# Broadcasting position rows in another stage, and clipping index scores in their banks

## The chip, the cores and the metric

The kernel runs on one core of one Trainium2 chip. The time is device microseconds of one execution. A core has a tensor engine (PE, whose weight loads are listed as PEld), a vector engine (DVE), a scalar engine (ACT), GpSimd (POOL), and SyncE (SP), which here only issues DMA. Each engine works through its own queue in order; semaphores tie the queues together. PE writes into eight banks of PSUM; everything else lies in SBUF or in device memory.

## The reference, cut to what matters

Three transformer blocks run one after the other on a 1024 x 1024 sequence in float32. Block one normalises its input, projects it, passes part of it through a depthwise convolution and a state-space scan, and does differential attention. Block two has a gated unit, a band attention, a memory attention, and a sparse attention (DSA) that keeps, for each query, the 256 best keys by an index score. Block three is a windowed attention beside a convolution, and an MLP. The change touches two computations.

The first is data that depends on relative position: for the band attention and for the sparse attention, a row of biases per head.

```python
s = jnp.where(valid[None, :, None, None, :, :], s + bias[None, None], -jnp.inf)   # band
bias = t5_table[t5_bucket(idx - qpos[None, :, None])]                             # sparse
```

The second is the index score, a weighted sum over eight index heads of the clipped product of an index query and the index keys:

```python
logits = jnp.einsum('bqhd,bsd->bqhs', iqb.astype(jnp.float32), ikf) * (IDX_DIM ** -0.5)
score = jnp.einsum('bqhs,bqh->bqs', jax.nn.relu(logits),
                   iwb.astype(jnp.float32) * (IDX_HEADS ** -0.5))
_, idx = lax.top_k(score, k_sel)
```

## The kernel before, in words

Every engine has one program: a list of stages (`gpsimd_program`, `sync_program` and so on at the end of the file), each stage a function such as `pe_norm` or `pool_conv`. Nothing is planned at run time; the order in each queue is the order in which the functions issue. Float32 products are made from three products of split parts: a matrix is split into a high part (ACT copies it) and a low part (DVE or POOL subtracts), and each product is hi x hi + hi x lo + lo x hi.

**DMA.** SP starts the loads and POOL the stores, through a class `Transfers` with eight lanes of semaphores each: transfer n waits, on the issuing engine, until transfer n-8 has landed. The order of all stores is written out in `store_order` so that any engine can wait for a named store.

**The norm stage** (`*_norm`). Eight tiles of 128 positions are normalised. Then z is projected in 16 pieces (`("nat", n)`, n = 0 to 15; product L688), which ACT takes out of the banks into four buffers and POOL stores (`saved(n)`, tensor `z_spill`). Beside the last of these PE makes the position rows (`pe_rows`), ACT takes them out, SP writes them to device memory (`("row", ...)`), and POOL broadcasts each row to 128 copies with a copy from device memory to device memory (`pool_rows`: `band_wide`, 1536 KB, and `toe_wide`, 2304 KB). The attention stages of block two read these wide tensors through a skewed pattern (`attention_tables`).

After the 16 pieces, v and g are projected with seven products in place of eight (`SEVEN`, product L735). The weights of each product come in two units. For unit u SP loads raw blocks (`sp_unit`, waits for PE's unit u-4, and for the first unit of kind 5, which is unit 4, for the z stores 12 to 15, whose buffers lie under the ones that it fills), POOL may subtract two blocks (`pool_unit`), ACT makes the high part (L385), DVE the low part (L394), PE multiplies: 24 matmuls per unit. Finished tiles of v and g are stored by POOL (`finished`), and all engines wait for the last of these stores before the next stage (`norm_over`).

**The convolution stage** (`*_conv`). Thirteen column tiles of 128 (items; `b1item_stage`) are loaded by SP, split (ACT L819, DVE L826), multiplied (L837, 48 matmuls each), taken out by ACT (L947), filtered by DVE with five taps (L1020 to L1024), passed through silu by ACT (L942), and transposed by PE (L211) and stored by POOL (`("xs", tile)`). At its beginning SP also loads small vectors, the memory input and its weights (`sp_memory`).

**The projections of block two with the index scores** (`*_two`). A fixed list `PLAN2` interleaves quarters of projections (PE L2659, 12 matmuls) with the 48 score units (query tile t = 2 to 7, index head h = 0 to 7), two after each quarter. For a score unit PE multiplies (t+1) x 128 keys into one of two pairs of banks (`K.pair[1 + n % 2]`), ACT clips it at zero into one of three SBUF buffers (L2810), and DVE multiplies it by the head's weight and adds it to the score tile `sel` (L3081 for the first head, L3084 for the others). PE waits for clip n-2 to reuse a pair, ACT for add n-3 to reuse a buffer. DVE also does, between the score units, the layer norm of the gated unit (L2838 to L2851) and a bisection for the 256th best key (counts, L2879). POOL makes low parts of weights (L2617). After the last scores come two products `mix` (PE L2793), both in the same pair of banks: the second waits until DVE has read the first (L3105).

Of the kernel before, what the change touches and what calls it, by code (L numbers as in the profile page):

```python
# [6 lines left out]
P = 128  # L7
# [731 lines left out]
def pool_norm(K):  # L739
    g, S, m = K.g, K.S, K.p1  # L740
    g.wait_ge(S["half"], 1)

    def saved(n):
        w, half = NAT[n // ST]
        g.wait_ge(S["nat_act"], n + 1)
        K.stores.start(g, ("nat", n), K.nat_dram[w][n % ST, :, half * 512:(half + 1) * 512], m.out[n % 4])

    for st in range(ST):
        g.wait_ge(S["ln_var"], st + 1)
        s = K.stat[st][:, 14:15]  # L750
        g.tensor_tensor(s, s, K.half, ALU.pow).then_inc(S["ln_rstd"], 1)
        if st:
            g.wait_ge(S["ln_h"], st)
            K.stores.start(g, ("h", st - 1), K.h_dram[(st - 1) * P:st * P, :], m.h[(st - 1) % 3])
        if st >= 3:
            saved(st - 3)
    g.wait_ge(S["ln_h"], ST)
    K.stores.start(g, ("h", ST - 1), K.h_dram[(ST - 1) * P:, :], m.h[(ST - 1) % 3])
    for n in range(ST - 3, NAT_N):
        saved(n)  # L760
        if n == NAT_N - 3:
            pool_rows(K)

    def finished(n):

        w, i = SEVEN[n]
        if i not in NAT_ENDS:
            return
        end = NAT_ENDS[i]
        if w == "v":  # L770
            g.wait_ge(S["nat_sum"], summed_at(w, end))
        else:
            g.wait_ge(S["nat_g"], list(NAT_ENDS).index(i) + 1)
        row, col = NAT_PLACE[end]
        K.stores.start(g, ("nat7", NAT_FINALS.index((w, end))), K.nat_dram[w][4 * row:4 * row + 4, :, col * 512:(col + 1) * 512].rearrange("s p n -> p s n"), nat_tile(K, w, end))

    for n in range(1, len(SEVEN)):
        pool_unit(K, 2 * n + 2)
        pool_unit(K, 2 * n + 3)
        if n >= 2:  # L780
            finished(n - 2)
    finished(len(SEVEN) - 2)
    finished(len(SEVEN) - 1)
# [256 lines left out]

def pool_conv(K):
    g, S, m = K.g, K.S, K.p2
    for tile in range(8):
        g.wait_ge(S["conv_out"], 2 + tile + 1)
        K.stores.start(g, ("xs", tile), K.xs_dram[:, :, tile * P:(tile + 1) * P].rearrange("s p n -> p s n"), m.xsT[tile % 2])
# [1355 lines left out]
def pool_rows(K):  # L2401

    for name, _, _ in ROW_KINDS:
        K.g.wait_ge(*K.loads[("row", name)])
        K.stores.start(K.g, ("wide", name), K.wide_dram[name], over(K.row_dram[name], 1, P))
# [343 lines left out]
def pe_two(K):  # L2749
    pe, S, m = K.pe, K.S, K.t2  # L2750
    pe.wait_ge(S["pj_hT"], ST)
    pe.wait_ge(S["pj_hlo"], ST)
    for x in range(FIRST2, 2 * FIRST2):
        for part in range(2):
            pe_half_quarter(K, x, part)
    for event in PLAN2:
        if event[0] == "q":
            pe_half_quarter(K, *event[1:])
        elif event[0] == "s":
            n = event[1]  # L2760
            t, h = IDX_UNITS[n]
            if n == 0:
                for i in range(FIRST2):
                    for part in range(2):
                        for to in range(2):
                            pe.wait_ge(*K.stores[("stack", i, part, to)])
            if n >= 2:
                pe.wait_ge(S["ix_relu"], n - 1)
            width = (t + 1) * P
            for x in range(0, width, 512):  # L2770
                w = min(512, width - x)
                last = products(pe, K.pair[1 + n % 2][:, x:x + w], [(m.iq[h][:, t * P:(t + 1) * P], k[:, x:x + w]) for k in m.ik])
            last.then_inc(S["ix_sc"], 1)
        elif event in MISC2:
            use = misc2(K, event)
            if use:
                pe.wait_ge(S["p1_read"], use)
            if event[0] == "iw":
                pe.wait_ge(S["p1_act"], HALF_AT[(0, 1)] + 1)
                for st in range(ST):  # L2780
                    last = pe.transpose(K.bank[6][:, st * IDX_HEADS:(st + 1) * IDX_HEADS], m.iwT[HD:HD + IDX_HEADS, st * P:(st + 1) * P], K.eye[HD:HD + IDX_HEADS, HD:HD + IDX_HEADS])
            elif event[0] == "t":
                n = ITEM_AT[event[1:]]
                pe.wait_ge(S["p1_act"], HALF_AT[(n, 1)] + 1)
                last = transposed(pe, K.pair[3], [row2(K, n, 0, False)[:, st * P:(st + 1) * P] for st in range(ST)], K.eye)
            else:
                kk = event[1]
                pe.wait_ge(S["sgu_vn"], ST)
                pe.wait_ge(S["sgu_ws"], 1)
                for st in range(ST):  # L2790
                    for r in range(2):
                        gr = 2 * kk + r
                        last = pe.matmul(K.pair[3][r * HD:(r + 1) * HD, st * P:(st + 1) * P], m.vn[:, st, gr * HD:(gr + 1) * HD], m.wsT[:, gr], start=True, stop=True)  # L2793
            last.then_inc(S["p1_turned"], 1)


def act_two(K):
    a, S, m = K.a, K.S, K.t2
    for x in range(FIRST2, 2 * FIRST2):
        act_half(K, x)  # L2800
    for event in PLAN2:
        if event[0] == "q" and event[2]:
            act_half(K, event[1])
        elif event[0] == "s":
            n = event[1]
            width = (IDX_UNITS[n][0] + 1) * P
            a.wait_ge(S["ix_sc"], n + 1)
            if n >= 3:
                a.wait_ge(S["ix_add"], n - 2)
            a.activation(m.relu[n % 3][:, 0:width], K.pair[1 + n % 2][:, 0:width], ACT.Relu).then_inc(S["ix_relu"], 1)  # L2810
        elif event[0] == "level":
            i, at = event[1], LEVELS2.index(event)
            k, t = K.kth[2 + i], SIGN_TILES[i]
            if at == 0:
                a.wait_ge(*K.stores[("b2y", 0)])
            a.wait_ge(S["kth_bound"], at + 1)
            if at:
                a.wait_ge(S["kth_count"], at)
            a.activation(m.mixed[0][:, 0:(t + 1) * P], K.sel[t], ACT.Sign, bias=k.bound, scale=-1.0, accum_out=k.n).then_inc(S["kth_count"], 1)
        elif event[0] in ("iw", "t"):  # L2820
            a.wait_ge(S["p1_turned"], misc2(K, event) + 1)
            if event[0] == "iw":
                a.activation(K.iw.rearrange("p s h -> p (s h)"), K.bank[6][:, 0:ST * IDX_HEADS], ACT.Copy, scale=(IDX_HEADS * HD) ** -0.5).then_inc(S["p1_read"], 1)
            elif event[1] == "v":
                i = event[2]
                a.activation(m.vn[:, :, i * P:(i + 1) * P], by_k(K.pair[3]), ACT.Copy).then_inc(S["p1_read"], 1)
            else:
                n = ITEM_AT[event[1:]]
                stage_free(K, a, n, 1)
                a.activation(row2(K, n, 1, False), K.pair[3], ACT.Copy).then_inc(S["p1_read"], 1)  # L2830
# [222 lines left out]
def dve_two(K, top):  # L3053
# [5 lines left out]
    for event in PLAN2:  # L3059
# [12 lines left out]
        elif event[0] == "s":  # L3072
            n = event[1]
            t, h = IDX_UNITS[n]
            width = (t + 1) * P
            r, wcol, sel = m.relu[n % 3][:, 0:width], K.iw[:, t, h:h + 1], K.sel[t]
            if n == 0:
                v.wait_ge(S["p1_read"], misc2(K, ("iw",)) + 1)
            v.wait_ge(S["ix_relu"], n + 1)
# [1799 lines left out]
def block_two_memory(nc, K):  # L4879
# [17 lines left out]
    m.stats, m.rstd = a.take("stats", [P, ST, 8]), a.take("rstd", [P, ST])  # L4897
    mid0 = -(-a.at // 512) * 512
    a = Space(nc, "b2mid", mid0, mid0 + 24 * 1024)
    m.relu, m.vn, mixed0 = a.several("relu", 3, [P, S_LEN]), a.take("vn", [P, ST, GW]), a.take("mixed0", [P, S_LEN])  # L4900
    a = Space(nc, "b2x", mid0, mid0 + 24 * 1024)
    m.hi_x, m.lo_x = a.several("hi", 3, [P, KT, P], F32R), a.several("lo", 3, [P, KT, P], F32R)
    ring0 = a.at
# [162 lines left out]
def store_order():  # L5066

    order = []
    for st in range(ST):
        order += [("h", st - 1)] * (st > 0) + [("nat", st - 3)] * (st >= 3)  # L5070
    order += [("h", ST - 1)] + [("nat", n) for n in range(ST - 3, NAT_N - 2)] + [("wide", name) for name, _, _ in ROW_KINDS] + [("nat", n) for n in range(NAT_N - 2, NAT_N)] + [("nat7", n) for n in range(len(NAT_FINALS))]
    order += [("xs", tile) for tile in range(8)]
    order += [("yb", ch) for ch in range(ST - 1, -1, -1)] + [("y", ch) for ch in range(ST)]
    order += [("ya", half) for half in range(2 * A_HEADS)] + [("b1p", st) for st in range(ST)]
    order += store_order_two() + [("b2y", k) for k in (2, 3, 6, 7)] + [("b2p", st) for st in range(ST)]
    for h in range(NH):
        order += [("win", h), ("win_in", h)]
    return order + [("x3", st) for st in range(ST)] + store_order_mlp()
# [145 lines left out]
```

## Time and profile before

| | us |
|---|---|
| median of 3 runs | 3033.34 |
| lowest and highest | 3030.15, 3034.22 |
| the profiled execution | 3033.2 |
| its span | 3031.9 |
| PE busy | 2867.9 (95%) |
| DVE busy | 2249.0 (74%) |
| ACT busy | 1271.5 (42%) |
| POOL busy | 720.4 (24%) |

The profiled execution is one run; its span goes from the first instruction to the last. Times in rows are microseconds from the start of the span unless they are marked ns. A line number is that of the program; `L133` is the line that starts any DMA. A bracket at the end of a row gives the engine's idle time before the instruction and who ended it.

### The profile page before, as it was taken

The numbers are of one execution on the slowest core, as the hardware profiler recorded it, in microseconds if no ns is written. First come the engines' busy times: TensorE is split into PE (matmuls) and PEld (weight loads), VectorE is DVE, ScalarE is ACT, GpSimd is POOL, SyncE is SP. The second block draws the span as 40 slices with busy tenths as digits, with TensorE's granted clock in tenths as the row PEclk, the third lists the DMA queues.
The fourth block names the chain that finished last, engine by engine and source line by source line (L and its number), as shares of the span: only waits on it lengthen the run. The fifth ranks groups of instructions, "written<-read, shape, count | busy, mean of one in ns | idle before, by whom it ended". The sixth has DMA issues, their size and how long they took to land. (4 is left out here: it accounts for less than half of the span.)

```text
span 3031.9 us, 39024 instructions
## 1 busy us (share of the span) xinstructions
PE 2867.9 (95%) x14496; PEld 2273.6 (75%) x14496; DVE 2249.0 (74%) x3445; ACT 1271.5 (42%) x2298; POOL 720.4 (24%) x561
## 2 busy tenths in 40 slices
PE   7999999999899999989899999999889999999999
PEld 6678876777688878867788777844567878887887
DVE  7355644599899964855998755889886767778888
ACT  2223331377678862223467576111364322223332
POOL 1032002355311110221134325010001143333221
PEclk9999999999899999999999999999999999999999
DMA  6345224544522316433137544231002233354331
GB/s 230 129 165 174 92 73 155 194 136 136 194 82 90 120 62 224 153 96 73 42 112 222 167 138 177 89 113 59 28 8 81 96 127 111 111 197 150 111 111 56
DMA packets 222333, 370.24 MB, mean 122 GB/s; under 512 B 19066, under 2 KB 120602, under 8 KB 222146
## 3 DMA queue, kind: packets, MB, share of 16 engines
q1 hardware_dynamic: 193378, 271.00, 27.3%
q0 software_dynamic: 28768, 96.76, 8.6%
q8 instruction: 116, 1.90, 0.3%
q14 instruction: 71, 0.58, 0.1%
HBM read 257.30 MB, written 109.08 MB: 121 GB/s over the span
## 5 line engine op out<-in xcount | busy, mean ns | idle before, releaser
L4589 PE MATMUL banks<-b3down_r_t 128*128 128x512 f32 x1344 | 307.4, 391 | 8.2 <-DVE b3down_r_t L4621 7.5
L4589 PEld LDWEIGHTS banks<-b3down_r_t 128*128 128x128 f32 x1344 | 253.6, 189 | 62.0 <-DVE b3down_r_t L4621 7.9
L837 PE MATMUL banks<-b_hThi,b1item_hi 128*128 128x512 f32 x464 | 194.8, 420 | 1.6 <-DVE b1ln_big L529 1.3
L4342 PE MATMUL banks<-b3up_t_t,b3up_w_w 128*128 128x512 f32 x768 | 182.9, 394 | 1.0 <-DVE b3up_w_w L4299 1.0
L2659 PE MATMUL banks<-b2h_hi,b2h_whi 128*128 128x512 f32 (+1 forms) x448 | 177.6, 396 | 4.8 <-DVE b2h_lo L2061 2.4
L837 PE MATMUL banks<-b_hThi,b1item_lo 128*128 128x512 f32 x464 | 181.7, 392 | 0.0
L837 PE MATMUL banks<-b_hTlo,b1item_hi 128*128 128x512 f32 x464 | 181.2, 391 | 0.0
L2659 PE MATMUL banks<-b2h_lo,b2h_whi 128*128 128x512 f32 (+1 forms) x448 | 176.0, 393 | 0.0
L2659 PE MATMUL banks<-b2h_hi,b2h_wlo 128*128 128x512 f32 (+1 forms) x448 | 176.0, 393 | 0.0
L4342 PEld LDWEIGHTS banks<-b3up_t_t,b3up_w_w 128*128 128x128 f32 x768 | 143.8, 188 | 36.1 <-DVE b3up_w_w L4299 2.5
L1757 DVE CUSTOM_DVE_ANT_0 b1att_map<-banks,b1att_dist 128x1024 f32<-128x1024 f32 x128 | 151.5, 1221 | 8.5 <-PE banks L1670 6.3
L1721 ACT ACTIVATE b1att_map<-b1att_map,fixed_stat 128x1024 f32<-128x1024 f32 x128 | 146.5, 1145 | 4.2 <-DVE fixed_stat L1757 4.2
L4606 ACT ACTIVATE b3down_r_t<-b3down_a_t 128x2048 fp32r<-128x2048 f32 x28 | 53.7, 1919 | 197.1 <-PE banks L4589 185.8
L3531 DVE SCALAR_TENSOR_TENSOR b3keep_acc<-b3conv_pad,b3conv_w,b3keep_acc 128x512 f32<-128x512 f32 (+1 forms) x120 | 122.2, 1018 | 4.0
L189 PE MATMUL banks<-b1att_vals,b1att_turned 128*128 128x128 f32 x1024 | 125.1, 275 | 0.0
L189 PEld LDWEIGHTS banks<-b1att_vals,b1att_turned 128*128 128x128 f32 x1024 | 119.4, 192 | 0.2
L1670 PE MATMUL banks<-b1att_k,b1att_q 64*128 64x512 f32 x768 | 107.2, 411 | 10.7 <-DVE fixed_stat L1757 10.7
L837 PEld LDWEIGHTS banks<-b_hThi,b1item_hi 128*128 128x128 f32 x464 | 87.8, 189 | 25.8 <-issue 7.3
L2617 POOL TENSOR_TENSOR b2h_wlo<-b2h_stage,b2h_whi 128x1024 fp32r<-128x1024 f32 x26 | 63.4, 2439 | 182.0 <-ACT b2h_whi L2600 181.9
L837 PEld LDWEIGHTS banks<-b_hTlo,b1item_hi 128*128 128x128 f32 x464 | 87.7, 189 | 23.8 <-issue 6.7
L2659 PEld LDWEIGHTS banks<-b2h_hi,b2h_whi 128*128 128x128 f32 (+1 forms) x448 | 84.3, 188 | 23.7 <-issue 6.5
L837 PEld LDWEIGHTS banks<-b_hThi,b1item_lo 128*128 128x128 f32 x464 | 87.4, 188 | 19.0
(614 smaller groups left out, 7496.7 us busy)
## 6 DMA issues: line engine op xcount, KB each, us to landing
b1raw_w<-in_w_in SPq DMA_DIRECT2D x32, 512.0 KB, 3.7
qk_spill<-b1scan_qk SPq DMA_DIRECT2D x64, 256.0 KB, 3.2
b1out_ws<-in_w_out SPq DMA_DIRECT2D x16, 1024.0 KB, 5.1
b3upr_raw<-in_w_mlp_up SPq DMA_DIRECT2D x16, 1024.0 KB, 5.2
b3down_a_t<-act_spill SPq DMA_DIRECT2D x16, 1024.0 KB, 6.1
b3down_b_t<-in_w_mlp_down SPq DMA_DIRECT2D x16, 1024.0 KB, 8.7
b2h_stage<-in_w_in SPq DMA_DIRECT2D x30, 512.0 KB, 4.0
b1item_stage<-in_w_in SPq DMA_DIRECT2D x29, 512.0 KB, 5.2
```

Source lines behind the costliest of these rows:

```text
L189: last = pe.matmul(out, lhsT, rhs, start=i == 0, stop=i == len(pairs) - 1)
L837: last = K.pe.matmul(pair[:, ss], a, b, start=q % 2 == 0 and i == 0, stop=q % 2 == 1 and i == 11)
L1670: last = pe.matmul(K.pair[1 + i][:, cols], q[rr, x, t * P:(t + 1) * P], k[rr, y, cols], start=n == 0, stop=n == 2)
L1721: a.activation(mp, mp, ACT.Exp, bias=s[:, i:i + 1], scale=-1.0, accum_out=s[:, 2 + i:3 + i]).then_inc(S["att_exp"], 1)
L1757: v.tensor_tensor_reduce(mp, K.pair[1 + i], m.dist[:, x0:x0 + S_LEN], -1.0, 3e38, ALU.add, ALU.min, s[:, i:i + 1]).then_inc(S["att_shift"], 1)
L2617: g.tensor_tensor(lo, m.stage[:, :, 0:w], hi, ALU.subtract).then_inc(K.S["w2_lo"], 1)
L2659: last = pe.matmul(K.bank[x % 2][0:w], a[:, k, 0:w], b[:, k, ss], start=part == 0 and i == 0, stop=part == 1 and i == 11)
L3531: last = v.scalar_tensor_tensor(acc, m.pad[i][:, x0 + j:x1 + j], m.convw[:, i, j:j + 1], acc, ALU.mult, ALU.add)
L4342: last = pe.matmul(out, y[:, 4 * half + k], z[:, k], start=c == 0, stop=c == 11)
L4589: last = pe.matmul(K.bank[b], x[:, q, cols], y[:, q], start=c == 0, stop=c == 11)
L4606: a.activation(d.ring[n % 2][0], side_a(K, g)[ROLE_A[i]], ACT.Copy).then_inc(S["down_hi"], 1)
```

## The change

POOL no longer broadcasts the position rows after z store 13, but at the beginning of `pool_conv`, behind all stores of the norm stage; the written-out order of stores follows. The index scores are clipped in place: ACT writes the clipped scores back into the banks, DVE reads them there, and PE reuses a pair of banks when DVE's add n-2 is done. ACT's wait for add n-3 goes. The three SBUF buffers stay allocated and unused.

```diff
 def pool_norm(K):
     for n in range(ST - 3, NAT_N):
         saved(n)
-        if n == NAT_N - 3:
-            pool_rows(K)
...
 def pool_conv(K):
     g, S, m = K.g, K.S, K.p2
+    pool_rows(K)
     for tile in range(8):
         g.wait_ge(S["conv_out"], 2 + tile + 1)
...
 def pe_two(K):
             if n >= 2:
-                pe.wait_ge(S["ix_relu"], n - 1)
+                pe.wait_ge(S["ix_add"], n - 1)
...
 def act_two(K):
+            scores = K.pair[1 + n % 2][:, 0:width]
             a.wait_ge(S["ix_sc"], n + 1)
-            if n >= 3:
-                a.wait_ge(S["ix_add"], n - 2)
-            a.activation(m.relu[n % 3][:, 0:width], K.pair[1 + n % 2][:, 0:width], ACT.Relu).then_inc(S["ix_relu"], 1)
+            a.activation(scores, scores, ACT.Relu).then_inc(S["ix_relu"], 1)
...
 def dve_two(K, top):
-            r, wcol, sel = m.relu[n % 3][:, 0:width], K.iw[:, t, h:h + 1], K.sel[t]
+            r, wcol, sel = K.pair[1 + n % 2][:, 0:width], K.iw[:, t, h:h + 1], K.sel[t]
...
 def store_order():
-    order += [("h", ST - 1)] + [("nat", n) for n in range(ST - 3, NAT_N - 2)] + [("wide", name) for name, _, _ in ROW_KINDS] + [("nat", n) for n in range(NAT_N - 2, NAT_N)] + [("nat7", n) for n in range(len(NAT_FINALS))]
+    order += [("h", ST - 1)] + [("nat", n) for n in range(ST - 3, NAT_N)] + [("nat7", n) for n in range(len(NAT_FINALS))] + [("wide", name) for name, _, _ in ROW_KINDS]
     order += [("xs", tile) for tile in range(8)]
```

## Rows read from the trace of the kernel before

**Rows 1.** The page's fourth part: the chain that ended last, by engine.
```profile
PE 34%; DVE 5%; ACT 2%; issue 1%; DMA 1%; POOL 1%; ACTq 0%; DVEq 0%; SPq 0%; POOLq 0%
```
**Rows 2.** Busy time by stretch: PE, PEld, DVE, ACT, POOL, granted clock, DMA share, GB/s.
```profile
124.00:146.00 22.00, 21.98 (x97) 17.85 (x96) 2.77 (x3) 4.29 (x3) 0.56 (x1) 1.00 0.39 153
157.00:160.00 3.00, 2.98 (x7) 2.42 (x8) 3.00 (x1) 0.86 (x1) 3.00 (x2) 0.50 0.29 111
```
**Rows 3.** Timeline of PE, 145 to 162: start, duration, instruction.
```profile
157.03 1.19 PE L735 MATMUL banks<-b1ln_w,b1ln_s1hi 128*128 128x512 f32 x2 [11.05 <-DVE b1ln_w L394]
...
161.68 0.61 PE L735 MATMUL banks<-b1ln_w,b1ln_s1hi 128*128 128x512 f32 x2
```
**Rows 4.** Busy time in the index-score stretch, columns as in rows 2.
```profile
1412.00:1502.00 90.00, 77.42 (x368) 63.00 (x366) 85.00 (x221) 37.74 (x46) 15.27 (x7) 0.98 0.13 36
```
**Rows 5.** Timeline of PE: the score of unit 28, the first and the second mix.
```profile
1444.99 0.85 PE L189 MATMUL banks<-b2idx_ik,b2idx_iq 128*128 128x512 f32 x4
...
1492.17 1.97 PE L2793 MATMUL banks<-b2ringr_wsT,b2mid_vn 128*64 128x128 f32 x32
...
1502.53 3.53 PE L2793 MATMUL banks<-b2ringr_wsT,b2mid_vn 128*64 128x128 f32 x32 [5.45 <-DVE b2mid_mixed L3105]
```
**Rows 6.** Timeline of SP: its first load for unit 4.
```profile
145.63 0.39 SPq L133 DMA_DIRECT2D b1ln_t<-in_w_in  x1
```
**Rows 7.** Timeline of POOL, 116 to 126.
```profile
116.59 1.09 POOL L133 DMA_DIRECT2D toe_wide<-toe_row  x1
...
125.15 0.56 POOL L133 DMA_DIRECT2D z_spill<-b1lnz_out  x1 [4.86 <-ACT b1lnz_out L619]
```
**Rows 8.** DMA issues of 100 to 115, then 117 to 144: KB, us to landing.
```profile
z_spill<-b1lnz_out POOLq DMA_DIRECT2D x3, 256.0 KB, 2.3
...
toe_wide<-toe_row POOLq DMA_DIRECT2D x1, 2304.0 KB, 27.6
z_spill<-b1lnz_out POOLq DMA_DIRECT2D x2, 256.0 KB, 22.8
```
**Rows 9.** DMA issues of 306 to 319.
```profile
b1item_stage<-in_w_in SPq DMA_DIRECT2D x1, 512.0 KB, 13.2
```
**Rows 10.** Timelines of ACT and PE in the convolution.
```profile
324.88 1.06 ACT L819 ACTIVATE b1item_hi<-b1item_stage 128x1024 fp32r<-128x1024 f32 x1
325.83 1.02 ACT L931 ACTIVATE b1ssm_B<-banks 128x1024 f32<-128x1024 f32 x1
331.09 1.16 ACT L942 ACTIVATE b1ssm_BT<-b1conv_acc,b1ssm_convb 128x1024 f32<-128x1024 f32 x1 [4.24 <-DVE b1conv_acc L1024]
...
336.33 1.03 PE L211 MATMUL banks<-fixed_eye,b1ssm_BT 128*128 128x128 f32 x8
```
**Rows 11.** Busy time in a stretch with the toe broadcast in flight, columns as in rows 2.
```profile
136.00:144.00 8.00, 8.00 (x37) 6.60 (x36) 0.00 (x0) 1.02 (x1) 0.00 (x0) 1.00 0.26 106
```
**Rows 12.** DVE lines: ns min/median/max; first without, then with a bank operand.
```profile
L1467 DVE TENSOR_TENSOR b1scan_state<-b1scan_state,b1ssm_carry x12: 1212/2065/2915, 503.6 to 762.6; 128x1024 f32<-128x1024 f32 x12
L1475 DVE TENSOR_TENSOR b1scan_state<-b1scan_state,banks x12: 1211/1217/1222, 506.9 to 769.2; 128x1024 f32<-128x1024 f32 x12
```
**Rows 13.** Timeline of DVE: add 25, a tile's first add, an undisturbed and a blocked pair.
```profile
1445.76 1.02 DVE L3084 SCALAR_TENSOR_TENSOR b2late_sel<-b2mid_relu,b2late_iw,b2late_sel 128x768 f32<-128x768 f32 x1
...
1481.24 0.75 DVE L3081 TENSOR_SCALAR b2late_sel<-b2mid_relu,b2late_iw 128x1024 f32<-128x1024 f32 x1
...
1485.10 2.67 DVE L3084 SCALAR_TENSOR_TENSOR b2late_sel<-b2mid_relu,b2late_iw,b2late_sel 128x1024 f32<-128x1024 f32 x2
...
1489.50 4.82 DVE L3084 SCALAR_TENSOR_TENSOR b2late_sel<-b2mid_relu,b2late_iw,b2late_sel 128x1024 f32<-128x1024 f32 x2
```
**Rows 14.** Timelines of POOL and DVE near 1360.
```profile
1359.49 2.37 POOL L2617 TENSOR_TENSOR b2h_wlo<-b2h_stage,b2h_whi 128x1024 fp32r<-128x1024 f32 x1 [6.02 <-ACT b2h_whi L2600]
...
1360.02 0.75 DVE L2701 SCALAR_TENSOR_TENSOR b2ringr_row<-banks,b2h_bcol,b2ringr_row 128x512 fp32r<-128x512 f32 x1 [10.51 <-ACT b2ringr_row L2687]
```
**Rows 15.** PE's waits in 1445 to 1500: us in total, times, longest.
```profile
PE banks L189 <- ACT b2mid_relu L2810: 2.0, 3, 1.0
```

More of the change, by code:

```diff
@@ L4899, in block_two_memory @@
     a = Space(nc, "b2mid", mid0, mid0 + 24 * 1024)
-    m.relu, m.vn, mixed0 = a.several("relu", 3, [P, S_LEN]), a.take("vn", [P, ST, GW]), a.take("mixed0", [P, S_LEN])
+    _, m.vn, mixed0 = a.several("relu", 3, [P, S_LEN]), a.take("vn", [P, ST, GW]), a.take("mixed0", [P, S_LEN])
     a = Space(nc, "b2x", mid0, mid0 + 24 * 1024)
```

## The prediction

> **What bounds the kernel now.** I read the chain of waits first: the reader is to see that the tensor engine (PE) carries 34% of the span on the chain that ended last, with DVE a distant 5% [rows 1]. So this is a PE-bound kernel, and an edit is worth what it does to PE's idle time and to its clock, no more. Then I looked for PE's idle time in the two stages that the diff touches, with the views by stretch and the timelines.
>
> In the norm stage PE runs without a gap up to 145.8 us (97 matmuls in 22 us, 0.227 us each), then stands for 11.05 us, and restarts at half clock [rows 2, 3]. In the index-score stage of block two DVE is busy 85.0 of 90 us and PE 77.4 [rows 4]; here DVE sets the pace, and PE waits for it at the end [rows 5].
>
> **Part one, the broadcasts leave the norm stage.** Why does PE stand at 145.8? It wants unit 4, whose parts DVE finishes just before 157. SP issues unit 4's loads only at 145.63 [rows 6], because `sp_unit` waits there for the z stores 12 to 15: the buffers of the seven-product stage lie over theirs. POOL issues the last of these at 125.15, behind the toe broadcast of 116.59 [rows 7]. An undisturbed z store lands in 2.3 us; the toe broadcast takes 27.6 us, that is until 144.2, and the two z stores issued behind it take 22.8 us in the middle [rows 8]. The last of them lands right before SP goes on at 145.63: it is the broadcast, through the store queue, that holds the loads.
>
> Without it, the last z store lands at about 125.15 + 0.6 + 2.3 = 128. The next condition is older: unit 4 reuses unit 0's raw buffer, so SP waits for PE's unit 0, which begins at 124.1 and has 24 matmuls: 129.5. From SP's issue to PE's first matmul is 157.03 - 145.63 = 11.4 us now, and unit 4 can be ready at 129.6 + 11.4 = 141, where PE wants it at 145.8: 4.8 us to spare. Unit 5's loads leave after unit 1 (135), unit 6's after unit 2 (140.4), each against a PE need three to four units (5.44 us each) later. What is late next is then nothing of this stage: SP's requests become spread by PE's units, as they are after 157 now.
>
> PE gets back 11.05 us and the slow restart. Its first twelve matmuls after the stall take from 157.03 to 161.68, 4.65 us, where twelve at 0.227 take 2.72: 1.9 us [rows 3]. The granted clock is 0.50 in 157 to 160, the lower of its two levels (1.2 of 2.4 GHz), after 11 us in which PE did nothing, against 1.00 before [rows 2]. Sum: 11.05 + 1.9, with rounding 13.0 us. DVE's and ACT's work of that stretch starts earlier and is not on the path. POOL's two issues (1.1 us each) cost nothing where they were: it waits for ACT between z stores.
>
> **The same broadcasts in the convolution.** POOL issues them behind the last g store, where it stands idle until the first x store. The g stores are ahead in its queue, so the stage boundary, which waits for them, is not held; nor is an x store, since both broadcasts have ended (27.6 us) long before the first of these: it follows the sixth item of 48 matmuls, each item 48 x 0.227 = 10.9 us. The store lanes are eight and their order is consistent: x store 6 waits for the band broadcast, ended by then. The tables are read only in block two.
>
> What they can hit is SP's traffic. On the clock of the trace before, the toe broadcast would run from 301.6 to 329.2. SP then fetches small vectors, the memory (1 MB), its weights (2 MB) and item 4, which lands 13.2 us after 306.2, at 319.4 [rows 9]. ACT takes item 4 at 324.88; ACT's silu for PE's transpose at 336.33 is behind that in ACT's queue [rows 10]. With the split at X, the silu ends at X + 0.95 + 1.02 + 1.16, so PE waits only if X is past 333.1. With the toe alone in flight the DMA share is 0.26, a quarter of the engines [rows 11]; a transfer of SP's lands when its last engine has finished. Bounds: below, no slowing, 319.4. Above, the shared engines serve SP only after the broadcast: 329.2 + 11 us of SP's work (13.2 less the 2 us that any transfer takes to land) = 340.2, so PE stands 340.2 - 333.1 = 7.1 us and pays another 1.9 us for its restart: 9.0 us. If time on them is halved, SP's 11 us take 22 from 306: 328, past ACT's 324.88 but short of 333.1, hidden by PE's items 3 and 4. I take that, 0 us, as nearest to what two busy queues would share; the upper end is kept for the range.
>
> The Trainium skill's page "DMA: Bandwidth & Descriptors" (section "Queues, rings and completion order") speaks against this half: an engine takes turns between its queues by whole packets, not by time. The broadcast's rows are 4608 bytes, item 4's are 512, and by that rule the small ones pay for the large: the sum would be near the upper end. No run here shows two such queues together.
>
> **Part two, the clipped scores stay in the banks.** It removes nothing from the count of instructions: 48 ACT clips, 48 DVE adds. ACT writes where it read; DVE reads the bank; PE's score n waits for DVE's add n-2 instead of ACT's clip n-2, and ACT no longer waits for add n-3. Behind the waiting score stand PE's next quarter of a projection (2.72 us) and everything after.
>
> DVE's price. An fp32 operation with a bank operand and 1024 columns takes 1.21 to 1.22 us [rows 12], not more than the add now (2.67 us for two undisturbed [rows 13]). The first operation of each tile now runs fast, 0.749 us for 1024 [rows 13]; from a bank I take 1.2. Four of them in the DVE-bound stretch: +0.4 us each, +1.6. Gain: three adds in that stretch coincide with a POOL subtraction and take about 2.1 us longer (4.82 us for two at 1489.50), one 0.4. Is that blocking gone when the operand is in a bank? The rows say so: an all-SBUF product reaches 2.9 us from 1.21 but the same shape with a bank operand never exceeds 1.222 [rows 12], and the very form of our add (bank, column, SBUF row) took 0.75 us inside POOL's 1359.49 to 1361.86 [rows 14]. So DVE gets back 6.6, net 5.0.
>
> PE's price. Up to score 27 DVE sets the pace. Walking the three queues with the durations of the trace, add 25, which ends at 1446.8 now [rows 13], ends at 1446.9 in the changed kernel too (DVE's norm and count work of 3.5 us and more between pairs sets its time there); score 27 then starts, takes 0.8 us, a quarter follows, so score 28 starts at 1450.6 instead of 1444.99 [rows 5]. From there DVE's pair of adds and counts (2.6 + 1.8 = 4.4 us) is shorter than PE's pair with its quarter (2.04 + 2.72 = 4.8 us at full width), and add n ends about 1.2 us before score n+2 wants it. PE runs through. Its pure time from score 28 to the second mix is 1502.53 - 5.45 - 1444.99 = 52.1, less 2.0 of waits for clips [rows 5, 15] = 50.1. So the second mix can start at 1450.6 + 50.1 = 1500.7, not 1502.53: 1.8 us. DVE must have taken the first mix by then: last add 1497.1, counts 2.0, read 1.2: 1500.3, just in time. And PE, no longer idle for 5.45 us before it, does the mix in 1.97 us and not 3.53 [rows 5]: 1.6 us. Sum 3.4 us. Bounds: if POOL's blocking stays, each blocked add passes on to PE past its 1.2 us of slack, the walk gives 1505.1, and with the fast mix 1.0 us is lost; if clips and adds both cost 0.06 us less, another 0.5 is won.
>
> **The sum** is made against the profiled execution: 3033.2 (span 3031.9 and 1.3 around it), within 0.2 us of the median 3033.34. 3033.2 - 13.0 + 0 - 3.4 = 3016.8.
>
> **Rivals.** (a) The broadcast starves item 4: 7.1 + 1.9 lost, 3025.8. For it: both bursts start within 4 us of each other, and SP's is 3.5 MB. Against: 12 of 16 engines are free. (b) POOL's blocking survives, because the add still reads an SBUF tile: 3033.2 - 13.0 + 1.0 = 3021.2. Against it [rows 12, 14]. The Trainium skill's "SBUF — State Buffer" (section "SBUF: two separate sides") gives the lock to a DVE operation with two SBUF inputs; the trace agrees for the forms above. (c) Slower than before: the turn through the banks. If clip and add in the same banks cost DVE twice its time, DVE's path grows by 32 adds of 1.1 us; my walk then puts the second mix at 1527.3, +24.8, so 3033.2 - 13.0 + 24.8 = 3045. It decides from about +0.67 us an add, where it eats the 13.0. Against: 1.21 us [rows 12]; for: no engine but PE writes a bank in the trace of before. (d) It does not do what it says: SP is held at unit 4 by something else, and both parts give nothing: 3033. Against: z stores of 2.3 us against 22.8.
>
> **Chances.** Forecast 0.62, (a) 0.17, (b) 0.10, both of them 0.02 (3030), (c) 0.03, (d) 0.03, other 0.03. About 6 us (0.2%) is what a measurement of this kernel can tell. Faster: 0.62 + 0.17 + 0.10 + a little of the rest = 0.90; same: (d), (a) with (b), 0.06; slower: (c) and half of other, 0.04. The likeliest case alone spans 3013 to 3021; (a) sets the upper end: 3012 to 3026.
>
> **What would show it.** After: no PE gap near 146, clock 1.00 through 160; z stores at 2 to 3 us; SP's unit 4 loads near 129.6. In the convolution: item 4 lands later than 13.2 us after issue, and no gap at the transpose 23 us behind it. In the scores: adds without a 2 us outlier; PE gaps of 4 to 5 us twice near the norm work, almost none after; the wait before the second mix under 1 us. Wrong would be: a gap in PE of over 3 us in the convolution, adds above 1.4 us, or unit 4 still waiting.

## The result and the profile after

The changed kernel takes 3017.6 us (median of 4 runs, 3016.55 to 3022.62) beside 3033.8 of the kernel before in the same session: 0.995 of it, interval 0.9938 to 0.9961. The forecast was 3016.8, range 3012 to 3026. The profiled execution took 3017.83, its span 3016.4. PE is busy 2865.6 us (95%), DVE 2240.1 (74%), ACT 1270.9, POOL 719.9: all within 0.5% of before, so again it is the idle time and the clock of PE that moved. Lines have shifted: L2810 of before is L2808, L3084 is L3082, L1020 is L1018, L942 is L940.

Both traces list the same 14,496 records of PE in the same order, so the start of a matmul can be set against the start of the same one before. That gives the whole account of these two traces (us):

| the same work of PE | before | after | difference | since the row above |
|---|---|---|---|---|
| a matmul of the first projections | 27.64 | 26.76 | -0.9 | -0.9 |
| item 0 of the convolution | 290.99 | 276.88 | -14.1 | -13.2 |
| item 1, behind the first transposes | 326.10 | 317.11 | -9.0 | +5.1 |
| the quarter behind score 15 | 1409.91 | 1399.02 | -10.9 | -1.9 |
| the quarter behind the second mix | 1505.99 | 1490.48 | -15.5 | -4.6 |
| end of the span | 3031.9 | 3016.4 | -15.5 | 0.0 |

**The norm stage.** The same two stretches as in [rows 2]: busy time of PE, PEld, DVE, ACT, POOL, then granted clock, DMA share, GB/s.

```profile
124.00:146.00 22.00, 22.00 (x99) 18.22 (x98) 6.47 (x6) 5.65 (x4) 7.00 (x4) 1.00 0.46 155
157.00:160.00 3.00, 3.00 (x15) 2.49 (x14) 1.58 (x2) 1.76 (x2) 0.58 (x1) 1.00 0.51 171
```

PE does 15 matmuls in 157 to 160 at clock 1.00, where it did 7 at 0.50. The timelines of SP and PE answer to [rows 3, 6]: SP's first load for unit 4, and PE's first matmul of it, with no idle time in a bracket.

```profile
128.72 0.40 SPq L133 DMA_DIRECT2D b1ln_t<-in_w_in  x1
```
```profile
144.85 0.62 PE L735 MATMUL banks<-b1ln_w,b1ln_s1hi 128*128 128x512 f32 x2
```

The z stores issued in 117 to 127 answer to the last of [rows 8]. They take 3.1 us (median) where they took 22.8:

```profile
z_spill<-b1lnz_out POOLq DMA_DIRECT2D x2, 256.0 KB, 3.1
```

**The convolution.** Here is a gap of PE that was not there. It is at the first transposes of the stage, one item ahead of those of [rows 10]; before the change these ran without a gap:

```profile
324.47 1.09 PE L211 MATMUL banks<-fixed_eye,b1ssm_BT 128*128 128x128 f32 x8
```

Timelines of ACT, DVE and PE after the change, with the idle time and its releaser in the bracket:

```profile
298.97 1.03 ACT L945 ACTIVATE b1conv_raw<-banks 128x1024 f32<-128x1024 f32 x1 [7.74 <-PE banks L835]
...
312.87 1.15 ACT L940 ACTIVATE b1ssm_BT<-b1conv_acc,b1ssm_convb 128x1024 f32<-128x1024 f32 x1 [11.92 <-DVE b1conv_acc L1022]
...
323.90 1.06 ACT L817 ACTIVATE b1item_hi<-b1item_stage 128x1024 fp32r<-128x1024 f32 x1 [8.97 <-DMA b1item_stage<-in_w_in]
```
```profile
306.80 0.75 DVE L1018 TENSOR_SCALAR b1conv_acc<-b1conv_raw,b1ssm_convw 128x1024 f32<-128x1024 f32 x1 [14.24 <-DMA b1ssm_convw<-in_conv_w_cols]
```
```profile
314.07 1.97 PE L211 MATMUL banks<-fixed_eye,b1ssm_BT 128*128 128x128 f32 x8 [3.64 <-ACT b1ssm_BT L940]
```

Read backwards: PE waits for ACT's silu, ACT for DVE's taps, DVE for the load of the tap weights `conv_w`. ACT had the input of the taps ready at 298.97 + 1.03 = 300.0; the weights landed at 306.8, 6.8 us later. PE stood 3.6 us of that, so the chain had 6.8 - 3.6 = 3.2 us to spare. The loads issued in 288 to 299 answer to [rows 9] (KB, us from issue to landing):

```profile
b1conv_wkv<-in_w_mem_kv SPq DMA_DIRECT2D x1, 2048.0 KB, 26.2
...
b1item_stage<-in_w_in SPq DMA_DIRECT2D x1, 512.0 KB, 25.0
b1ssm_convw<-in_conv_w_cols SPq DMA_DIRECT2D x1, 30.0 KB, 15.2
b1ssm_bias<-in_dt_bias_fwd SPq DMA_DIRECT2D x1, 8.0 KB, 7.0
```

A vector of 30 KB takes 15.2 us; before the change it took 4.1:

```profile
b1ssm_convw<-in_conv_w_cols SPq DMA_DIRECT2D x1, 30.0 KB, 4.1
```

Item 4 takes 25.0 us where it took 13.2. The single DMA packets in the trace say more than the durations. The tap weights are 128 packets of 240 bytes: 64 start between 295.4 and 296.7, the other 64 only between 301.7 and 306.2. `band_wide` lands at 306.59 and the tap weights at 306.77, and in each of the four other traces with the copies as they are and in this place the tap weights also land 0.2 to 0.4 us behind `band_wide`.

PE stands 3.64 us and then restarts slowly: the eight transposes take 1.97 us in place of 1.09, and the granted clock of 314 to 316 is 0.50, the lower of the two levels. Together 5.1 us.

**The index scores.** The seven full-width adds of the last tile, DVE's groups by form (us in all, mean ns), and below them all 42 adds, min/median/max:

```profile
L3082 DVE SCALAR_TENSOR_TENSOR b2late_sel<-banks,b2late_iw,b2late_sel 128x1024 f32<-128x1024 f32 x7 | 9.0, 1283 | 1.0 <-ACT banks L2808 0.5
```
```profile
L3082 DVE SCALAR_TENSOR_TENSOR b2late_sel<-banks,b2late_iw,b2late_sel x42: 617/949/1284, 1373.5 to 1483.3; 128x384 f32<-128x384 f32 x7, 128x512 f32<-128x512 f32 x7, 128x640 f32<-128x640 f32 x7, 128x768 f32<-128x768 f32 x7
```

In the trace before the seven full-width adds have a mean of 1590 ns, and the longest of the 42 takes 3429:

```profile
L3084 DVE SCALAR_TENSOR_TENSOR b2late_sel<-b2mid_relu,b2late_iw,b2late_sel x42: 617/1016/3429, 1384.4 to 1497.4; 128x384 f32<-128x384 f32 x7, 128x512 f32<-128x512 f32 x7, 128x640 f32<-128x640 f32 x7, 128x768 f32<-128x768 f32 x7
```

PE's waits in 1371 to 1505 (us in all, times, longest) and the second mix, for [rows 5, 15]:

```profile
PE banks L189 <- DVE b2late_sel L3079: 4.4, 2, 3.5
PE banks L189 <- DVE b2late_sel L3082: 4.0, 3, 3.5
```
```profile
1488.58 1.97 PE L2792 MATMUL banks<-b2ringr_wsT,b2mid_vn 128*64 128x128 f32 x32
```

PE now waits early, twice 3.5 us near DVE's norm work, and not at all before the mix, where it stood 5.45 us. One clash is left there, and the change doesn't touch it: a norm operation with two SBUF operands is held by the same kind of subtraction, while the seven others of its kind take 0.42 to 0.48 us:

```profile
1412.23 2.38 POOL L2616 TENSOR_TENSOR b2h_wlo<-b2h_stage,b2h_whi 128x1024 fp32r<-128x1024 f32 x1
```
```profile
1412.39 2.52 DVE L2847 SCALAR_TENSOR_TENSOR b2mid_vn<-b2mid_vn,b2late_stats,b2idx_g 128x256 f32<-128x256 f32 x1 [1.89 <-POOL b2late_rstd L3141]
```

### The profile page after: what moved, and what is told of

Same layout as the page of the kernel before. It is cut to its first block and busy times, and to the rows that moved or that the text cites. A ratio compares the mean times of both kernels' runs of the same rounds, so it can differ in the third digit from the quotient of the medians.

```text
span 3016.4 us, 38979 instructions
## 1 busy us (share of the span) xinstructions
PE 2865.6 (95%) x14496; PEld 2271.2 (75%) x14496; DVE 2240.1 (74%) x3445; ACT 1270.9 (42%) x2298; POOL 719.9 (24%) x561
```

## The experiments

Theory at the outset: the z stores queued behind the broadcasts made the norm stall; the broadcasts starve SP's loads in the convolution; adds that read a bank aren't held by POOL's subtractions. Rivals: the two parts depend on each other, the convolution's gap is an older limit reached earlier, the score gain is the new order of waits. Ratios are to the kernel before on the same chip, whose medians were 3033.7 to 3036.1.

### The two parts alone

`e1_rows_alone` keeps only the edits of `pool_norm`, `pool_conv` and `store_order`; `e2_banks_alone` only those of the scores.

> Part one alone: the broadcasts at the start of the convolution, the index scores as before. Theory (from the two traces): the norm stage gives 13.0 us, the convolution takes 5.1 back (3.6 us of idle PE and a slow restart of about 1.5), so about 8 us under the kernel before, near 3025.5, and no gap of PE near 146. The sum of the prediction had 13.0 and nothing given back: 3020.5. Rival, the two parts lean on each other (the tables or the clock reach into the score stage): further than 3 us from 3025.5. PE's wait at the first transposes of the convolution should be 3 to 4 us, on ACT's silu, with conv_w landing over 10 us after its issue.

> Part two alone: the scores clipped in the banks, the broadcasts in the norm stage as before. Theory: 4.4 us (the second mix starts without a wait and at full clock), near 3029.3; the 11 us gap of PE near 146 is still there. Prediction: 3.4 us, 3030.3. Rival, that the score stage gained only because PE reached it earlier or at a better clock: under 2 us, 3032 or more. The adds should have a mean of 1.28 us at 1024 columns with none above 1.35.

Part one: 3025.7 us, 0.997 (0.996 to 0.998). Part two: 3029.2, 0.9982 (0.9973 to 0.9991). Both lie within 0.2 us of what the traces had led to, and 8.6 and 5.1 us under the 3034.3 of their session make 13.7 of the 14.8 to 16.2 measured for both. If the parts lean on each other, it is by less than this noise. The waits of PE, part one in 120 to 340, part two in 120 to 170:

```profile
PE banks L211 <- ACT b1ssm_BT L940: 4.1, 1, 4.1
```
```profile
PE banks L735 <- DVE b1ln_w L394: 12.4, 1, 12.4
```

### The broadcasts somewhere else

`e3_rows_attention`: in the differential attention.

```diff
 def pool_att(K):
         if u >= 8 and u % 4 == 0:
             half_saved(K, u // 4 - 2)
+            if u == 20:
+                pool_rows(K)
```

> Both parts, but the broadcasts moved on into the differential attention of block one, behind the store of its fourth half head (about 907 us), where the DMA engines are busy a quarter of the time. Theory (the 5.1 us lost in the convolution are contention of the broadcasts with SP's loads there, and nothing else): the convolution runs as before the change, no gap of PE at its first transposes, and 5 us less than the changed kernel: 3012.6. In the attention stores behind the broadcasts on POOL's queue take 20 to 25 us instead of 2.3, and loads of 3.6 to 7 us may double; both have 36 us of room, so nothing is lost. Rival 1, the attention has less room than that: a gap of 3 to 10 us moves there, 3015 to 3022. Rival 2, the gap in the convolution has another cause (an earlier arrival of PE at a DVE or SP limit that was always there): no change against the changed kernel, 3017.6.

3020.1 us, 0.995 (0.9937 to 0.9962): the convolution has no gap and wins 5.1 us against the changed kernel's trace, but PE loses 6.0 us near 939, 5.4 of them idle. So rival 2 fell and rival 1 came true. The waits in 900 to 960, and the DMA issues of 900 to 935, say how:

```profile
ACT b1att_yT L1726 <- DMA yT_spill<-b1att_yT: 6.0, 1, 6.0
...
PE banks L1686 <- ACT b1att_junk L1708: 5.4, 1, 5.4
```
```profile
toe_wide<-toe_row POOLq DMA_DIRECT2D x1, 2304.0 KB, 29.9
...
b1att_g<-g_spill SPq DMA_DIRECT2D x1, 512.0 KB, 17.4
```

The yT store that POOL issued at 921.93, behind the broadcasts, landed at 936.92, one microsecond after the last of them; ACT waited for its buffer. It is the norm stall again, a store behind a long copy in one queue: the last 16 of its 64 packets start only at 934 to 936.2, as the toe copy ends (935.98). A load of SP's queue that was issued at 918.82 beside the same copies took 17.4 us, so another queue was slowed there too. My "36 us of room" was wrong; there were about 15.0 - 6.0 = 9.

`e4_rows_behind_z`: in the norm stage still, but behind z store 15.

```diff
     for n in range(ST - 3, NAT_N):
         saved(n)
+    pool_rows(K)
```

> Both parts, but the broadcasts stay in the norm stage, right behind the last z store (about 125 us) and ahead of the v and g stores. This takes the z stores out from behind the broadcasts and nothing else. Theory Q (the 11 us stall came from the stores queued behind the broadcasts; the broadcasts also slow what SP loads beside them, by about the factor seen in the convolution, 1.5 to 3.7): SP issues unit 4 at 129 and not 145, but its loads of 3.5 to 4.3 us take 8 to 16, so unit 4 is ready 4 to 12 us later than 140.6, against a need at 144.8: a PE gap of 0 to 8 us near 145. The convolution is clean (4.4 us won there). Time 3012.5 to 3021, middle 3017. Rival (with 12 of 16 DMA engines free the loads are not slowed): no gap, 3013. Rival (the stall was the broadcasts' use of the DMA engines and not the queue): a gap of 8 us or more, over 3021.

3023.5 us, 0.9969 (0.9958 to 0.9981). SP did issue unit 4 at 129.2, so what had held its issue was the place of the z stores behind the copies. But now the loads pay. The issues of 125 to 142, and PE's waits:

```profile
b1raw_w<-in_w_in SPq DMA_DIRECT2D x4, 512.0 KB, 16.2
...
b1ln_t<-in_w_in SPq DMA_DIRECT2D x2, 512.0 KB, 11.6
```
```profile
PE banks L735 <- DVE b1ln_w L394: 6.9, 3, 3.8
```

These loads take 3.4 to 4.3 us in the changed kernel, and 9.9 to 20.0 here. The time is 2.5 us above the upper end of my range, since units 5 and 6 were late too. Matmul against matmul with the changed kernel, PE loses 9.6 us between 144 and 165, 6.9 of them waiting and the rest in slow restarts. "12 of 16 engines are free" was no cover for these loads.

### What it is in the convolution

`e5_rows_after_taps` puts `g.wait_ge(*K.loads["conv_b"])` ahead of `pool_rows(K)` in `pool_conv`; `e6_rows_after_item4` puts `g.wait_ge(*K.loads[("item", 4)])` there.

> Both parts, but in the convolution POOL waits for the landing of the small vector conv_b before it broadcasts (about 6 to 8 us later). This spares the small vectors and lets the memory, its weights and item 4 meet the broadcasts. Theory V (only the starved tap weights cost PE time): the gap is gone, 3012.6. Theory I (item 4 is starved too and lies right behind: it landed at 323.9 in the changed kernel and PE, if it had not stood before, would have wanted it by about 319.0): the gap moves by one transpose and is 3 to 5 us, the time stays within 2 us of the changed kernel, 3016 to 3019.

> Both parts, but in the convolution POOL broadcasts only when item 4 has landed (about 305.5 us); SP loads nothing more until 335 us, and the first x store comes near 360. Theory: the whole burst of SP is spared, item 4 lands 13.2 us after its issue and not 25, no engine waits for a load there; the convolution gives back nothing: 3013 to 3015, the same as with the wait for conv_b (3015.2), where item 4 landed just in time. If it is more than 3 us under that, item 4 still cost something there.

3015.2 us (0.9931, 0.9918 to 0.9943) and 3014.7 (0.9939, 0.9926 to 0.9951). In both PE has no gap at its transposes. The first one decides between the vectors and item 4, because item 4 is as slow as ever in it (issues of 288 to 300):

```profile
b1item_stage<-in_w_in SPq DMA_DIRECT2D x1, 512.0 KB, 26.7
b1ssm_convw<-in_conv_w_cols SPq DMA_DIRECT2D x1, 30.0 KB, 4.2
```

Item 4 landed at 319.97. The prediction's limit for it, 333.1 on the clock of before, is 320.1 here (PE is 13.0 us earlier at this point). It was met by 0.1 us, and PE did not wait: ACT's silu ended at 323.00 and the transposes began at 323.37. That is theory V, with theory I just short of true. Against the first trace of the changed kernel both win 5.1 us in the convolution and have lost 3.5 and 3.8 of it by 500: by a slower restart near 419, and between 480 and 500, where PE waits 6.6 us for DVE's scan state and not 5.6. But these losses can't be put down to the edit: the changed kernel's own second trace (`e12_changed_again`) has them too, 1.6 us near 419, and a wait of 6.8.

`e9_rows_spread` leaves the broadcasts where the change put them and turns their loops round:

```diff
-        K.stores.start(K.g, ("wide", name), K.wide_dram[name], over(K.row_dram[name], 1, P))
+        K.stores.start(K.g, ("wide", name), K.wide_dram[name].rearrange("n p l -> p n l"), over(K.row_dram[name], 0, P))
```

> Both parts as changed, the broadcasts in the same place, but each copy walks the 128 rows in its outer loop and the 4 heads in its inner one, in place of 4 heads outside and 128 rows inside; bytes, packets and destination are the same. In the trace the copies with 4 outside use 4 of the 16 DMA engines for 19 to 28 us. Theory (the outer loop is what is dealt out to the engines, and what starves SP is how long a shared engine is shared): with 128 outside all 16 engines work, the two broadcasts end 12 to 15 us after they start instead of 35, before most of SP's small vectors are issued; conv_w lands under 8 us after its issue, the gap of PE goes or falls under 1 us: 3013 to 3015. Rival (the copies still go to 4 engines): nothing changes, 3017.6. Rival (all 16 engines shared is worse for SP than 4): the last g stores and the vectors land later than before, a longer gap, over 3019.

3014.6 us, 0.9938 (0.9925 to 0.9952). Issues of 281 to 300, the changed kernel first, then this one:

```profile
toe_wide<-toe_row POOLq DMA_DIRECT2D x1, 2304.0 KB, 35.2
...
band_wide<-band_row POOLq DMA_DIRECT2D x1, 1536.0 KB, 23.2
```
```profile
toe_wide<-toe_row POOLq DMA_DIRECT2D x1, 2304.0 KB, 17.5
...
band_wide<-band_row POOLq DMA_DIRECT2D x1, 1536.0 KB, 10.2
...
b1ssm_convw<-in_conv_w_cols SPq DMA_DIRECT2D x1, 30.0 KB, 12.4
```

The copies take half the time, and the DMA share near 290 is 1.01 (288 to 294) where it was 0.58 (289 to 295). The tap weights are still slow (12.4 us, over the 8 that I expected), yet land at 302.25. By the 3.2 us of slack found above they were due at 303.1, or 301.6 on this run's clock (1.5 us earlier): a gap of 0.65 us. PE's wait is 0.6.

### The same copies, spread, in two more places

`e10_spread_norm` has them between z stores 13 and 14 as before the change, `e11_spread_item4` behind item 4, both with the scores in the banks; `e12_changed_again` is the changed kernel beside them.

> Part two, and the broadcasts back in the norm stage, between z stores 13 and 14, but spread (128 rows in the outer loop of each copy, 4 heads inside), so that they last 17.5 us and not 28. Theory (the norm stall is the time that z stores 14 and 15 stand behind the broadcasts on POOL's queue): the broadcasts end near 134, the z stores with them, SP issues unit 4 at about 134.5 and not 145.6, the unit is ready 11.4 us later at 146 against a need at 145: a PE gap of 0 to 1.5 us in place of 11.05. The convolution has no broadcast and loses nothing. Time 3012.5 to 3015. Rival (the stall is the bytes that the broadcasts move, on all engines, or something else in SP's path): a gap of more than 5 us, over 3019.

> Both parts, the broadcasts in the convolution behind the landing of item 4, and spread over the engines. Theory: with the unspread copies behind item 4 nothing was lost in the convolution any more, so spreading can win nothing further: the same as that kernel (3014.7), within 1.5 us. The broadcasts should end near 320 and item 5 land in 3.6 us instead of 7.8. If it is faster by over 2 us, something in the convolution or the scan still waited for the long broadcasts.

> The changed kernel once more, on the chip of the two kernels beside it, for their comparison: 3017.6, within 1 us, and 3 to 4 us above the kernel with the spread broadcasts behind item 4.

3015.8 us (0.9938, 0.9924 to 0.9951), 3014.6 (0.9932, 0.9920 to 0.9945), 3019.3 (0.9951, 0.9938 to 0.9963). The first has the copies in the old place, with the same bytes and the same queue, only shorter, and the stall of 11.05 us is gone. Its issues of 112 to 136:

```profile
toe_wide<-toe_row POOLq DMA_DIRECT2D x1, 2304.0 KB, 14.7
...
z_spill<-b1lnz_out POOLq DMA_DIRECT2D x3, 256.0 KB, 7.2
```

The last z store lands at 130.41, SP issues unit 4 at 130.55, and PE has no wait there.

Why a z store behind the copies is late can be read from single packets of the trace before. The two z stores issued behind the copies are 128 packets of 4096 bytes. Of these, 64 start within 2 us of their issues, 32 between 133.7 and 135.6, when `band_wide` ends (134.17), and the last 32 between 143.0 and 144.9, when `toe_wide` ends (144.23). So half of each store went at once, and each quarter stood behind one of the copies until that had ended. SP issued no load between 113.9 and 145.6, so there was no other traffic of its queue to blame. In the trace before the stores land 0.7 and 1.3 us behind `toe_wide`, in this run 0.6 and 1.3.

The five versions at 3014.6 to 3015.8 can't be told from one another; the one with spread copies behind item 4 has no gap in the convolution and is 4.7 us under the changed kernel on the same chip. These are the fastest complete versions found.

### The score stage

`e7_coupled_sbuf` is part one with `pe.wait_ge(S["ix_add"], n - 1)` in `pe_two`, the clipped scores still in SBUF.

> Part one, and of part two only its wait: PE's score n waits for DVE's add n-2, while the clipped scores still lie in the three SBUF buffers. It is part one alone (3025.7) with the tighter coupling. Theory (what part two gains is that DVE's operand lies in a bank, where POOL's subtractions cannot block the add; the coupling by itself costs): the blocked adds of 3 to 4 us stay, PE passes them on, and the second mix comes 1 to 4 us later than in part one alone: 3026 to 3030. My walk of the three queues says 1505.1 instead of 1502.5 with 1.6 us won back at the mix: +1.0, 3026.7. Rival (the gain comes from the order of the waits, PE no longer running ahead): as fast as both parts, 3018 to 3021.

3028.5 us, 0.9983 (0.9974 to 0.9992), 2.8 us over part one alone. The two kernels ran on different chips and their intervals overlap, so the medians alone don't show a cost. They do exclude the rival, 3018 to 3021: the order of waits is not the gain. In the trace the scores up to the quarter behind the second mix take 1.5 us longer than in part one alone, matmul against matmul. PE waits 10.6 us for adds; the 42 adds:

```profile
L3083 DVE SCALAR_TENSOR_TENSOR b2late_sel<-b2mid_relu,b2late_iw,b2late_sel x42: 617/1018/2608, 1375.3 to 1491.6; 128x384 f32<-128x384 f32 x7, 128x512 f32<-128x512 f32 x7, 128x640 f32<-128x640 f32 x7, 128x768 f32<-128x768 f32 x7
```

`e13_short_subtractions` is part one alone, with POOL's subtractions beside the score units cut to 128 of their 1024 columns. It leaves out seven eighths of these low parts, so its result is not that of the other kernels:

```diff
-def pool_item2(K, n):
+def pool_item2(K, n, ks=KT):
...
-    g.tensor_tensor(lo, m.stage[:, :, 0:w], hi, ALU.subtract).then_inc(K.S["w2_lo"], 1)
+    g.tensor_tensor(lo[:, 0:ks], m.stage[:, 0:ks, 0:w], hi[:, 0:ks], ALU.subtract).then_inc(K.S["w2_lo"], 1)
...
-                pool_item2(K, item)
+                pool_item2(K, item, 1)
```

> Part one alone (3025.7), scores in SBUF buffers and the waits of before, but POOL's subtractions of weights beside the score units work on 128 of their 1024 columns; seven eighths of those low parts are left out. It is made to see whether these subtractions are what holds the adds. Theory: no add above 1.4 us (3.43 us was the longest before), DVE's path is shorter by the 6.6 us of the four held adds, PE's wait before the second mix (5.5 us) shrinks to under 1.5 us and the mix runs in 2 us: 4 to 7 us less than part one alone, 3019 to 3022, so all that the banks bring and more. Rival (the adds are held by something else, ACT or DMA): adds of over 2.5 us stay, 3025 to 3027.

3013.2 us, 0.9926 (0.9912 to 0.9939), 12.5 under part one alone and 6 below the range that I gave. The adds:

```profile
L3083 DVE SCALAR_TENSOR_TENSOR b2late_sel<-b2mid_relu,b2late_iw,b2late_sel x42: 617/950/1285, 1378.0 to 1482.9; 128x384 f32<-128x384 f32 x7, 128x512 f32<-128x512 f32 x7, 128x640 f32<-128x640 f32 x7, 128x768 f32<-128x768 f32 x7
```

No add is held, and an add from SBUF costs what one from a bank costs (1285 and 1284 ns at most): the subtraction was what was in the way. Matmul against matmul with part one alone, 10.0 us come between 1410 and the quarter behind the second mix and 3.2 behind that, where a wait of PE of 3.5 us (near 1709) is gone as well. What the short subtractions free there I have not followed. That it wins more in the scores than the banks do (10.0 and 4.6 us) has two visible causes: the first adds of the tiles keep their 0.42 to 0.75 us, where from the banks they take 0.62 to 1.28, and the norm operation that takes 2.52 us in the changed kernel takes at most 0.59. How the difference divides between them is open.

## Why the prediction was right, and where it was not

The total was 0.8 us off (2.5 against the second measurement of the same kernel, 3019.3), but not each term. The three terms with a cause sum to -12.7 us in the two traces, where the forecast had -16.4. So that the total came out so near is luck. Against the account at the top:

**Norm stage, -13.0: measured -13.2.** The links held: the queue, the issue of unit 4 (129.6 forecast, 128.72 measured), the need (145.8, and 144.85 on a clock 0.9 us earlier), the restart. Moving the broadcasts only behind the z stores would not have done: the loads were starved in that run (9.6 us).

**Convolution, 0: measured +5.1.** The step that failed is "What they can hit is SP's traffic", in three ways. It took item 4 for what would be late, and never asked who waits for the small vectors ahead of it; `conv_w` had 3.2 us to spare, landed 6.8 us behind the other input of the taps, and PE stood 3.64 us. It reckoned with the toe broadcast alone, a quarter of the engines (0.26), ending 27.6 us after its issue; both copies were in flight until 306.59, the DMA share was 0.58, and the toe broadcast took 35.2. And "if time on them is halved" was too kind to the small vectors: 4.1 us became 15.2; item 4's 13.2 became 25.0, nearly the doubling that was taken. The prediction's own sign of being wrong, a gap of PE of over 3 us in the convolution, came true. The bound 0 to 9.0 held the value. For item 4 itself nothing speaks against the limit of 333.1: a landing 0.1 us ahead of it cost nothing. The page's rule that spoke against this half (the Trainium skill, "DMA: Bandwidth & Descriptors", section "Queues, rings and completion order": turns by packets, not by time) agrees in direction: the 30 KB in packets of 240 bytes became 3.7 times as slow, item 4 in packets of 512 bytes 1.9 times. Whether the turns are of the size that it says, these traces don't show.

**Scores, -3.4: measured -4.6.** The mechanism was right: no add over 1.284 us, gaps early and none before the mix, the mix in 1.97. The first add of a tile takes 1.28 us at 1024 columns, not the 1.2 taken; so do the undisturbed adds, and the mean over seven fell from 1.59. The surplus is in the walk: its 1500.7, on the new clock (10.9 us earlier), is 1489.8, and the mix began at 1488.58. Rival (b), held adds with the new coupling, is what `e7_coupled_sbuf` is, and it costs 1.5 us in the trace and 2.8 by the medians, not 1.0; that is within the noise of the medians. The Trainium skill's "SBUF — State Buffer" (section "SBUF: two separate sides") has the two-input DVE operation and GpSimd lock each other out; an add of up to 3.43 us, and of at most 1.285 with the subtractions cut short, agrees.

**-0.9 and -1.9 that no step had.** The first is the start of the kernel: the same matmul begins anywhere between 25.2 and 28.8 in the fourteen traces, and 0.9 us later in the changed kernel's second trace than in its first. The second shows mostly in two places where PE restarted slowly before and not after, at 428 (clock 0.68 against 1.00) and at 1362 (0.80 against 1.00). It is no effect of the change either: over the same stretch the changed kernel's second trace is 1.6 us longer than the one before the change. That these 2.8 us cancelled half the convolution's loss is the luck.

**Rivals.** (a), the starved loads, was the nearest: its mechanism is real, its victim another. (c) is out: an add from the banks costs DVE no more than an undisturbed one from SBUF, and only the first of each tile pays (1.28 us for 0.75). (d) is out: SP issued unit 4 at 128.72.

## What to carry to other kernels

A long copy costs in two ways that the trace shows apart: whatever is queued behind it on its own queue lands after it (within 1.3 us of its end here), and loads from other queues slow down, in the convolution by 1.9 to 3.7 times, even where the DMA share is only 0.58. Before moving such a copy, list every wait on a load or store that it overlaps, smallest ones included, with the slack of each; and first see whether its outer loop can be turned so that it takes half the time, which made the old place as good as the new one. An elementwise operation that now and then takes two or three times its usual time is worth a look at what GpSimd does then: an operand in a bank removed the clash here, and the tighter coupling alone gained nothing.

## What the runs showed of the hardware that I had not expected

- The same bytes in the same rows between two places in device memory took 27.6 us with 4 as the outer loop and 14.7 with 128 (23.2 and 10.2 for the smaller one in the convolution, beside other traffic). The Trainium skill gives the rule ("DMA: Bandwidth & Descriptors", section "Why a DMA increments its semaphore by 16 and not by 1": the number of engines follows from the size of the slowest loop); the shares of 0.58 and 1.01 agree. I had read the 0.26 of [rows 11] and not drawn the consequence.
- A short stop of PE does not always cost the same. After 2.88 us of idle time the granted clock of the next 4 us was 0.68 before and 1.00 after. The second stretch of each kernel below is the one that follows the stop:

```profile
424.00:428.00 4.00, 1.44 (x9) 1.44 (x10) 3.86 (x6) 3.09 (x5) 0.00 (x0) 0.90 0.00 0
428.00:432.00 4.00, 4.00 (x13) 3.17 (x13) 3.65 (x3) 3.47 (x3) 0.89 (x1) 0.68 0.29 86
```
```profile
416.00:420.00 4.00, 2.45 (x15) 2.19 (x16) 3.89 (x4) 3.40 (x6) 0.00 (x0) 1.00 0.00 0
420.00:424.00 4.00, 4.00 (x20) 3.28 (x19) 2.64 (x3) 2.17 (x2) 0.89 (x1) 1.00 0.49 139
```

  All fourteen traces have the same stop. The 20 matmuls from the first transpose on take 3.7 us in five of them and 5.0 to 5.3 in nine. The changed kernel is in both groups, with its first and its second trace. So a single profile carries an uncertainty of 1.5 us from this place alone. What tips it stays open.
- A transfer can be late in part: half of each z store's packets went at once, and the rest only as the two copies ahead of it ended, one after the other.
